# RWKV scan: the inverse of each tile built on its transpose alone, one 64x64 turn per level, on one Trainium2 core

## The chip, the cores and the metric

One core of one Trainium2 chip. The metric is the device time of one execution in microseconds (us), lower is better. The kernel before takes 3937.26 us, the median of 3 runs (3935.75 to 3940.57).

## What is computed

The reference is a two-layer model (D = 1024, 512 tokens and 256 context tokens, batch 1), all in float32. The change touches one part, the RWKV-7 scan of the first layer:

```python
def wkv7_scan(s0, r, w, kk, a, k, v):
    def step(s, inp):
        r_t, w_t, kk_t, a_t, k_t, v_t = inp
        s_kk = einsum('bhvk,bhk->bhv', s, kk_t)
        s = (s * w_t[:, :, None, :] - s_kk[..., None] * (kk_t * a_t)[:, :, None, :]
             + v_t[..., None] * k_t[:, :, None, :])
        return s, einsum('bhvk,bhk->bhv', s, r_t)
```

It runs over 16 heads of 64, in both directions of time: first over the 256 context tokens from a zero state, then over the 512 tokens from the state that the context left.

## The kernel before, in words

**Stages.** The kernel is a row of stages, each a block in which every engine has its own program and waits on named semaphores. Only `stage_rwkv_scan` (L666 to L1255) is touched. It lies between the key directions (L595) and the output of the mixer (from L1265).

**Tiles.** The scan works on 12 tiles of 128 tokens: tiles 0 to 3 are the context, 4 to 11 the tokens (`is_lat`). Even tiles run forward and odd ones backward. A tile holds 2 chunks of 64 tokens (`c` or `rows_of(c)`, the two halves of the 128 partitions) and 16 heads, which are kept in two groups `g` of 8. So every per-tile matrix of scores is 32 blocks of 64x64, in a tile buffer of 128 x 16 x 64.

**The inverse.** In each chunk the recurrence needs T = (I - A)^-1, where A is strictly triangular (its side depends on the direction). The kernel before forms A (`scores(kappa, beta, 0, n)`, L981) and its transpose AT (L983), in PSUM banks 0, 1 and 2, 3. `start_of_inverse` (L1105) cuts out of them the start of T and of its transpose TT for blocks of 2, and AT; GpSimd adds the identity to T and to TT (L1098, L1101). Five levels (`LEVELS`, blocks of 2, 4, 8, 16, 32) then double the block. One level is four steps:

- `level_product` (L824): per group 16 matmuls of 64x64x64, AT by T, into bank g.
- `level_mask` (L1121): VectorE multiplies the bank by the mask of this level's blocks and writes X.
- `level_change` (L837): per group 32 matmuls with 32 columns each, half of them for the change of T (L847, not on the last level) and half for the change of TT (L850).
- `level_update` (L1127): VectorE adds the change to T (not on the last level) and to TT, 256 columns each.

Group 1 of a step runs while VectorE works on group 0.

**Other work of a tile.** On TensorE: the scores BT, and QT and GT for `is_lat` tiles (`scores`, L809); 24 turns of 128x128 (`turn`, L818); the projections of the next tile (`prep_decay` L855, `prep_rate` L865, `prep_sums` L873); `b_times_v` (L884); state work of the tile before (`from_state`, `to_state`, and for `is_lat` tiles `output_from_state` and `output_from_tile`); at the end `kappa_times_t` (L957) and `t_times_bv` (L967). On ScalarE (L1038 to L1091), in this order: copies of the three turned matrices (L1042), tanh of the next tile's projections (L1047, L1051), the copy of b_times_v's result (`bv`, L1081), `prep_factor` (L1055, which releases `tmp_ready`), `prep_exp` (L1061), and the copies `tkt` (L1088) and `ub` (L1090). On VectorE, `prep_rates` (L1144) waits for `tmp_ready`.

**What sets the order.** Every engine's order of work is written out by hand: TensorE at L976 to L1036, VectorE at L1205 to L1255. Within an engine nothing overtakes. SyncE (L775) loads a tile's inputs; the load of tile n+2 starts when `featured` (L1167) says that VectorE has finished the features of tile n+1.

Of the kernel before, what the change touches and what calls it, by code (L numbers as in the profile page):

```python
# [665 lines left out]
def stage_rwkv_scan(k, y):  # L666
# [3 lines left out]
    LEVELS = (2, 4, 8, 16, 32)  # L670
# [4 lines left out]
    with ExitStack() as s:  # L675
# [17 lines left out]
        AT, BT, T, TT, X = (sb(n, [P, 2 * HP, C]) for n in ("AT", "BT", "T", "TT", "X"))  # L693
# [8 lines left out]
        a_ps, at_ps, bt_ps, qt_ps, gt_ps = sem("a_ps"), sem("at_ps"), sem("bt_ps"), sem("qt_ps"), sem("gt_ps")  # L702
        turned, tok_taken = sem("turned"), sem("tok_taken")
        t_off, tt_off, t_ready, tt_ready = sem("t_off"), sem("tt_off"), sem("t_ready"), sem("tt_ready")
# [64 lines left out]
        def side_of(m, b, side):  # L769
            return m.rearrange("p (n s b) -> p n s b", s=2, b=b)[:, :, side, :]  # L770

        BEFORE = ("c_before0", "c_before1")

        with nc.Block() as block:
# [33 lines left out]
            def _(pe):  # L808
# [27 lines left out]

                def level_change(n, l):  # L837
                    b, d = LEVELS[l], n % 2
                    for g in range(2):
                        need(pe, masked, 2 * NL * n + 2 * l + g + 1)  # L840
                        if l == 0:
                            need(pe, tt_ready, 2 * n + g + 1)
# [133 lines left out]
                for n in range(-1, TILES + 1):  # L976
                    now, nxt, prev = 0 <= n < TILES, n + 1 < TILES, n >= 1
                    if now:
                        need(pe, featured, n + 1)
                        need(pe, updated, 2 * NL * n)  # L980
                        scores(kappa, beta, 0, n).then_inc(a_ps, 1)  # L981
# [5 lines left out]
                        turn(ktil, 6)  # L987
                        need(pe, tok_taken, 3 * n + 1)
                        turn(kappa, 4)
                        level_product(n, 0)  # L990
                        need(pe, tt_off, 2 * n + 2)
                        scores(ktil, kappa, 2, n).then_inc(bt_ps, 1)
                        if is_lat(n):
                            need(pe, tok_taken, 3 * n + 2)
                            scores(beta, rr[n % 3], 6, n).then_inc(qt_ps, 1)
                        level_change(n, 0)
                    if nxt:
                        prep_decay(n + 1)
                    if now:
                        if is_lat(n):  # L1000
                            need(pe, bt_sb, n + 1)
                            scores(ktil, rr[n % 3], 2, n).then_inc(gt_ps, 1)
                        level_product(n, 1)
                    if nxt:
                        prep_rate(n + 1)
                    if now:
                        b_times_v(n)
                        level_change(n, 1)
                    if nxt:
                        prep_sums(n + 1)  # L1010
                    if now:
                        level_product(n, 2)
                    if prev:
                        from_state(n - 1, 0)
                    if now:
                        level_change(n, 2)
                    if prev:
                        to_state(n - 1, 0)
                    if now:
                        level_product(n, 3)  # L1020
                    if prev:
                        from_state(n - 1, 1)
                    if now:
                        level_change(n, 3)
                    if prev:
                        to_state(n - 1, 1)
                        if is_lat(n - 1):
                            output_from_state(n - 1)
                    if now:
                        level_product(n, 4)  # L1030
                        level_change(n, 4)
                    if prev and is_lat(n - 1):
                        output_from_tile(n - 1)
                    if now:
                        kappa_times_t(n)
                        t_times_bv(n)  # L1036
# [56 lines left out]
            @block.gpsimd  # L1093
            def _(pool):
                for n in range(TILES):
                    for g in range(2):
                        need(pool, t_off, 2 * n + g + 1)
                        pool.tensor_tensor(group(T, g), group(T, g), wide("c_ident", 0), ALU.add).then_inc(t_ready, 1)  # L1098
                    for g in range(2):
                        need(pool, tt_off, 2 * n + g + 1)  # L1100
                        pool.tensor_tensor(group(TT, g), group(TT, g), wide("c_ident", 0), ALU.add).then_inc(tt_ready, 1)  # L1101

            @block.vector
            def _(dve):
                def start_of_inverse(n):  # L1105
                    d = n % 2
                    need(dve, a_ps, n + 1)
                    for g in range(2):
                        dve.tensor_tensor(group(T, g), bank8(g), wide("c_off1", 1 - d), ALU.mult).then_inc(t_off, 1)
                    need(dve, at_ps, n + 1)  # L1110
                    for g in range(2):
                        dve.tensor_tensor(group(AT, g), bank8(2 + g), wide(BEFORE[d], 1), ALU.mult).then_inc(at_sb, 1)
                    for g in range(2):
                        dve.tensor_tensor(group(TT, g), bank8(2 + g), wide("c_off1", d), ALU.mult).then_inc(tt_off, 1)
# [12 lines left out]
                def level_update(n, l):  # L1127
                    b, d = LEVELS[l], n % 2
                    for g in range(2):
                        need(dve, change_ps, 2 * NL * n + 2 * l + g + 1)  # L1130
                        for m, side, at0 in ((T, d, 0), (TT, 1 - d, 256)):
                            if m is T and l == NL - 1:
                                continue
                            cols = group(m, g).rearrange("p h (n s b) -> p h n s b", s=2, b=b)[:, :, :, side, :]
                            change = k.ps[:, g, at0:at0 + 256].rearrange("p (h n b) -> p h n b", h=HP, b=b)
                            ins = dve.tensor_tensor(cols, cols, change, ALU.add)
                        ins.then_inc(updated, 1)
# [67 lines left out]
                for n in range(-1, TILES + 1):  # L1205
                    now, nxt, prev = 0 <= n < TILES, n + 1 < TILES, n >= 1
                    if now:
# [3 lines left out]
                        kept(BT[:, :, :], 2, n, 1, bt_sb)  # L1211
                        if is_lat(n):
                            need(dve, qt_ps, outputs(n))
                            kept(QT[:, n % 2, :, :], 6, n, 0, qt_sb)
                        level_update(n, 0)
# [3 lines left out]
                        level_mask(n, 1)  # L1219
# [6 lines left out]
                    if now:  # L1226
                        level_mask(n, 2)
                    if prev:
                        add_from_state(n - 1, 0)
                    if now:  # L1230
                        level_update(n, 2)
# [4 lines left out]
                    if now:  # L1236
                        level_mask(n, 3)
# [4 lines left out]
                    if now:  # L1242
                        level_update(n, 3)
                    if nxt:
                        prep_rr(n + 1)
                    if now:
                        level_mask(n, 4)
                    if prev:
                        new_state(n - 1, 1)
                    if nxt:  # L1250
                        prep_ktil(n + 1)
                    if now:
                        level_update(n, 4)
                    if prev and is_lat(n - 1):
                        add_output(n - 1)  # L1255

# [2269 lines left out]
```

## Time and profile before

| | |
|---|---|
| median of 3 runs | 3937.26 us |
| the profiled execution | 3941.41 us |
| its span, first to last instruction | 3939.4 us |
| TensorE busy in the span | 3295.8 us (84%) |
| VectorE busy | 1126.9 us (29%) |
| ScalarE / GpSimd busy | 542.5 / 166.5 us |
| mean granted TensorE clock | 0.903 of full |
| the scan, 465 to 1180 us of the span | 715 us |

PE is TensorE's matmul side, PEld its weight load, DVE VectorE, ACT ScalarE, POOL GpSimd, SP SyncE; a trailing q is an engine's sequencer. One float32 matmul of the program stands in the trace as two MATMUL records with a LDWEIGHTS each, one transpose as one. The time in brackets at the end of a row is how long the engine sat idle before it, and what released it; "issue" is a wait for nothing that the profile shows.

### The profile page before, as it was taken

The numbers are of one execution on the slowest core, as the hardware profiler recorded it, in microseconds if no ns is written. First come the engines' busy times: TensorE is split into PE (matmuls) and PEld (weight loads), VectorE is DVE, ScalarE is ACT, GpSimd is POOL, SyncE is SP. The second block draws the span as 40 slices with busy tenths as digits, with TensorE's granted clock in tenths as the row PEclk, the third lists the DMA queues.
The fourth block names the chain that finished last, engine by engine and source line by source line (L and its number), as shares of the span: only waits on it lengthen the run. The fifth ranks groups of instructions, "written<-read, shape, count | busy, mean of one in ns | idle before, by whom it ended". The sixth has DMA issues, their size and how long they took to land. (4 is left out here: it accounts for less than half of the span.)

```text
span 3939.4 us, 75830 instructions
## 1 busy us (share of the span) xinstructions
PE 3295.8 (84%) x34311; PEld 2300.8 (58%) x34311; DVE 1126.9 (29%) x1926; ACT 542.5 (14%) x995; POOL 166.5 (4%) x167
## 2 busy tenths in 40 slices
PE   3898599989988899998599999995796678887774
PEld 1354488988882344444399999894344444544442
DVE  1301455655545211134511111012103473201102
ACT  0001222222202100001100010100101131100001
POOL 0000011010100000000100000001000010100000
PEclk8899699999997899998799999997896589899997
DMA  7722311011103122471467778661300011899994
GB/s 310 218 71 74 89 48 48 26 48 46 29 19 129 43 64 85 113 271 44 145 226 265 266 249 280 232 225 65 104 25 1 21 38 79 340 427 426 427 427 180
DMA packets 246763, 613.04 MB, mean 156 GB/s; under 512 B 27188, under 2 KB 136278, under 8 KB 230968
## 3 DMA queue, kind: packets, MB, share of 16 engines
q1 hardware_dynamic: 219720, 531.05, 37.0%
q10 hardware_dynamic: 15968, 54.41, 3.6%
q0 software_dynamic: 10768, 22.87, 1.9%
q8 instruction: 268, 4.39, 0.5%
q14 instruction: 39, 0.32, 0.0%
HBM read 565.64 MB, written 42.63 MB: 154 GB/s over the span
## 5 line engine op out<-in xcount | busy, mean ns | idle before, releaser
L2667 PE MATMUL ps<-moe_xt,moe_wb 128*128 128x152 f32 (+1 forms) x3520 | 456.6, 292 | 2.3 <-DVE moe_xt L2829 2.3
L2667 PEld LDWEIGHTS ps<-moe_xt,moe_wb 128*128 128x128 f32 x3520 | 451.9, 193 | 2.9 <-issue 2.1
L1633 PE MATMUL ps<-ffn_h,ffn_wb 128*128 128x512 f32 x704 | 304.2, 595 | 15.5 <-PEq L1539 15.5
L2347 PE MATMUL ps<-hier_wb,hier_xt 128*64 128x256 f32 x2048 | 244.3, 394 | 75.0 <-DMA hier_wb<-in_expert_w_up 43.7
L2347 PEld LDWEIGHTS ps<-hier_wb,hier_xt 128*64 128x64 f32 x2048 | 160.9, 142 | 170.1 <-issue 64.5
L1633 PEld LDWEIGHTS ps<-ffn_h,ffn_wb 128*128 128x128 f32 x704 | 134.4, 191 | 185.3 <-issue 185.3
L2674 PE MATMUL ps<-moe_hT,moe_wb 128*128 128x152 f32 (+1 forms) x1760 | 227.2, 290 | 0.0
L2674 PEld LDWEIGHTS ps<-moe_hT,moe_wb 128*128 128x128 f32 x1760 | 222.7, 190 | 0.0
L850 PE MATMUL ps<-TT,X 64*64 64x32 f32 x3840 | 213.2, 220 | 3.2 <-issue 2.3
L850 PEld LDWEIGHTS ps<-TT,X 64*64 64x64 f32 x3840 | 197.7, 136 | 4.5 <-issue 3.3
L847 PE MATMUL ps<-X,TT 64*64 64x32 f32 x3072 | 188.3, 220 | 3.7 <-issue 3.1
L847 PEld LDWEIGHTS ps<-X,TT 64*64 64x64 f32 x3072 | 173.9, 136 | 4.1 <-issue 2.9
L1702 PE MATMUL ps<-ffn_g,ffn_wd 128*128 128x512 f32 x352 | 153.0, 598 | 2.6 <-PEq L1605 2.6
L2363 PE MATMUL ps<-hier_wb,hier_actT 128*64 128x512 f32 x512 | 116.9, 598 | 17.0 <-DMA hier_wb<-in_expert_w_down 12.3
L833 PE MATMUL ps<-T,AT 64*64 64x64 f32 x3840 | 127.3, 219 | 0.0
L833 PEld LDWEIGHTS ps<-T,AT 64*64 64x64 f32 x3840 | 119.9, 134 | 7.1 <-issue 5.7
L2950 PE MATMUL ps<-in_u,in_wb 128*128 128x512 f32 x256 | 113.0, 604 | 10.0 <-PEq L2877 10.0
L1702 PEld LDWEIGHTS ps<-ffn_g,ffn_wd 128*128 128x128 f32 x352 | 67.4, 192 | 88.2 <-issue 88.2
L2833 DVE SCALAR_TENSOR_TENSOR moe_th<-moe_th,ps 128x152 f32<-128x152 f32 (+1 forms) x110 | 33.9, 308 | 286.1 <-ACT moe_th L2767 286.1
L462 DVE SCALAR_TENSOR_TENSOR mix<-xx,vec,h 128x768 f32<-128x768 f32 (+1 forms) x48 | 43.6, 969 | 203.3 <-PE ps L530 152.7
L1124 DVE TENSOR_TENSOR X<-ps,sq 128x512 f32<-128x512 f32 x120 | 81.2, 689 | 65.3 <-PE ps L833 63.5
L1661 DVE SCALAR_TENSOR_TENSOR ffn_th<-ffn_th,ps 128x512 f32<-128x512 f32 x22 | 15.2, 689 | 273.1 <-ACT ffn_th L1646 273.1
(486 smaller groups left out, 4129.6 us busy)
## 6 DMA issues: line engine op xcount, KB each, us to landing
moe_wb<-in_moe_w SPq DMA_DIRECT2D x60, 2048.0 KB, 10.3
hier_wb<-in_expert_w_gate SPq DMA_DIRECT2D x32, 2048.0 KB, 37.8
hier_wb<-in_expert_w_up SPq DMA_DIRECT2D x32, 2048.0 KB, 37.5
hier_wb<-in_expert_w_down SPq DMA_DIRECT2D x32, 2048.0 KB, 38.4
moe_wb<-in_moe_w SPq DMA_DIRECT2D x30, 1536.0 KB, 8.1
wb_ada<-in_ada_w SPq DMA_DIRECT2D x8, 3072.0 KB, 18.6
ada_late<-in_ada_w ACTq DMA_DIRECT2D x8, 3072.0 KB, 9.6
ffn_wb<-in_ffn_w SPq DMA_DIRECT2D x22, 1024.0 KB, 7.8
```

Source lines behind the costliest of these rows:

```text
L462: return dve.scalar_tensor_tensor(mix[:, n % 2, c, own], xx[:, c, own], k.v(f"mu{order[n]}")[:, c:c + 1], h[:, c, own], ALU.mult, ALU.add)
L833: mm = pe.matmul(k.ps[rows_of(c), g, q * C:(q + 1) * C], AT[rows_of(c), g * HP + q, :], T[rows_of(c), g * HP + q, :], start=True, stop=True)
L847: pe.matmul(k.ps[rows_of(c), g, q * 32:(q + 1) * 32], TT[rows_of(c), at, :], side_of(X[rows_of(c), at, :], b, d), start=True, stop=True)
L850: mm = pe.matmul(k.ps[rows_of(c), g, 256 + q * 32:256 + (q + 1) * 32], X[rows_of(c), at, :], side_of(TT[rows_of(c), at, :], b, 1 - d), sta ...
L1124: dve.tensor_tensor(group(X, g), bank8(g), wide(f"c_off{LEVELS[l]}", 1 - n % 2), ALU.mult).then_inc(masked, 1)
L1633: mm = pe.matmul(k.ps[:, bank + q, :], wb[:, j, q, c, o * P:(o + 1) * P], h[:, c, :], start=c == 0, stop=c == KC - 1)
L1702: mm = pe.matmul(k.ps[:, j, :], wd[:, j, c, :], g[:, c, :], start=c == 0, stop=c == FC - 1)
L2347: mm = pe.matmul(k.ps[both_halves(a), bank, 0:256], xs[:, c, :], wb[:, slot, at:at + 256], start=c == 0, stop=c == KC - 1)
L2363: mm = pe.matmul(k.ps[both_halves(a), 7, :], at_sb[:, c, :], wb[:, slot, at:at + 512], start=c == 0, stop=c == 3)
L2667: mm = pe.matmul(k.ps[:, bank, 0:width], wb[:, slot, at:at + P], xs[:, c, :], start=c == 0, stop=c == KC - 1)
L2674: mm = pe.matmul(out_columns(o, width), wb[:, slot, at:at + P], hT[:, f, 0:width], start=f == 0 and o % 3 == 0, stop=f == FC - 1 and (o % ...
L2950: mm = pe.matmul(k.ps[:, e % 6, :], own[:, piece] if kind == "fm" else tokens[:, piece], tokens if kind == "fm" else own, start=c == 0, st ...
```

## The change

The change drops T and keeps the recursion on AT alone. Six levels (blocks of 1 to 32) now do the same four steps: turn the current AT (`level_turn`: for the first half of the partitions a transpose, for the second a matmul with the identity), mask the turned matrix into X, multiply X by AT into the bank (64 columns a block), and add the whole bank to AT. The last level adds to TT, which GpSimd has filled with AT + I after level 4. The scores A, the start of T and TT, and GpSimd's additions to T go. The hand-written orders of TensorE and VectorE are rearranged around the six levels; ScalarE's is not.

```diff
-    LEVELS = (2, 4, 8, 16, 32)
+    LEVELS = (1, 2, 4, 8, 16, 32)
...
-                def level_product(n, l):
+                def level_turn(n, l):
                     for g in range(2):
                         if l == 0:
                             need(pe, at_sb, 2 * n + g + 1)
-                            need(pe, t_ready, 2 * n + g + 1)
                         else:
                             need(pe, updated, 2 * NL * n + 2 * (l - 1) + g + 1)
                         for q in range(HP):
-                            for c in range(2):
-                                mm = pe.matmul(k.ps[rows_of(c), g, q * C:(q + 1) * C], AT[rows_of(c), g * HP + q, :],
-                                               T[rows_of(c), g * HP + q, :], start=True, stop=True)
+                            cols, m, one = slice(q * C, (q + 1) * C), AT[:, g * HP + q, :], k.square("c_ident")[:, 0:C]
+                            pe.transpose(k.ps[rows_of(0), g, cols], m[rows_of(0), :], one[rows_of(0), :])
+                            mm = pe.matmul(k.ps[rows_of(1), g, cols], m[rows_of(1), :], one[rows_of(1), :], start=True,
+                                           stop=True)
                         mm.then_inc(x_ps, 1)
...
                         for q in range(HP):
                             at = g * HP + q
-                            if l < NL - 1:
-                                for c in range(2):
-                                    pe.matmul(k.ps[rows_of(c), g, q * 32:(q + 1) * 32], TT[rows_of(c), at, :],
-                                              side_of(X[rows_of(c), at, :], b, d), start=True, stop=True)
                             for c in range(2):
-                                mm = pe.matmul(k.ps[rows_of(c), g, 256 + q * 32:256 + (q + 1) * 32],
-                                               X[rows_of(c), at, :], side_of(TT[rows_of(c), at, :], b, 1 - d),
-                                               start=True, stop=True)
+                                mm = pe.matmul(k.ps[rows_of(c), g, q * C:(q + 1) * C], X[rows_of(c), at, :],
+                                               AT[rows_of(c), at, :], start=True, stop=True)
                         mm.then_inc(change_ps, 1)
```

TensorE's order of a tile after the change, with the functions' names (those in brackets only where the tile, or the one before, is an `is_lat` one):

```text
scores AT (waits ub_taken of the tile before), turn beta, turn ktil, level_turn 0, turn kappa,
scores BT, level_change 0, [scores QT], prep_decay, level_turn 1, [scores GT], prep_rate,
level_change 1, b_times_v, level_turn 2, prep_sums, level_change 2, from_state 0, level_turn 3,
to_state 0, level_change 3, from_state 1, level_turn 4, to_state 1, level_change 4,
[output_from_state], level_turn 5, [output_from_tile], level_change 5, kappa_times_t, t_times_bv
```

GpSimd and VectorE:

```diff
                 for n in range(TILES):
+                    need(pool, ub_ps, n)
                     for g in range(2):
-                        need(pool, t_off, 2 * n + g + 1)
-                        pool.tensor_tensor(group(T, g), group(T, g), wide("c_ident", 0), ALU.add).then_inc(t_ready, 1)
-                    for g in range(2):
-                        need(pool, tt_off, 2 * n + g + 1)
-                        pool.tensor_tensor(group(TT, g), group(TT, g), wide("c_ident", 0), ALU.add).then_inc(tt_ready, 1)
+                        need(pool, updated, 2 * NL * n + 2 * (NL - 2) + g + 1)
+                        pool.tensor_tensor(group(TT, g), group(AT, g), wide("c_ident", 0), ALU.add).then_inc(tt_ready, 1)
...
                 def level_update(n, l):
-                    b, d = LEVELS[l], n % 2
                     for g in range(2):
                         need(dve, change_ps, 2 * NL * n + 2 * l + g + 1)
...
+                        if l == NL - 1:
+                            need(dve, tt_ready, 2 * n + g + 1)
+                        m = group(AT if l < NL - 1 else TT, g)
+                        dve.tensor_tensor(m, m, bank8(g), ALU.add).then_inc(updated, 1)
```

In VectorE's order `level_update` 2 to 5 and `level_mask` 3 to 5 each have a place of their own. `prep_rates` still stands between `level_update` 1 and `level_mask` 2, `prep_rr` and `prep_ktil` now stand between `level_update` 4 and `level_mask` 5, and `level_update` 5 comes last, behind `add_output`.

## Rows read from the trace of the kernel before

**Rows 1.** The scan as one stretch: us, busy of PE, PEld, DVE, ACT, POOL; PEclk, DMA, GB/s.
```profile
465.00:1180.00 715.00, 653.25 (x20960) 617.63 (x20960) 395.34 (x648) 174.94 (x325) 59.92 (x48) 0.95 0.15 39
```

**Rows 2.** Groups by line, 429 to 1190 us: count, busy, mean ns, idle before.
```profile
L850 PE MATMUL ps<-TT,X 64*64 64x32 f32 x3840 | 213.2, 220 | 3.2 <-issue 2.3 <-DVE X L1124 0.9
L847 PE MATMUL ps<-X,TT 64*64 64x32 f32 x3072 | 188.3, 220 | 3.7 <-issue 3.1 <-DVE X L1124 0.6
L1124 DVE TENSOR_TENSOR X<-ps,sq 128x512 f32<-128x512 f32 x120 | 81.2, 689 | 65.3 <-PE ps L833 63.5
L814 PE MATMUL ps<-x 64*64 64x64 f32 x2304 | 51.9, 243 | 30.6 <-issue 21.4 <-DVEq L1167 8.2 <-ACT ub L1090 0.9
```

**Rows 3.** Timeline of TensorE: start, length, line, count.
```profile
940.85 1.16 PE L814 MATMUL ps<-rr,x 64*64 64x64 f32 x64
...
588.37 2.08 PE L892 MATMUL ps<-V,BT 64*64 64x64 f32 x64
594.09 2.06 PE L879 MATMUL ps<-sq,lw 64*128 64x128 f32 x32
```

**Rows 4.** Timeline of ScalarE in tile 2, same columns.
```profile
590.76 1.02 ACT L1081 ACTIVATE bv<-ps 128x1024 f32<-128x1024 f32 x1
591.68 3.17 ACT L1057 ACTIVATE x<-x,kar,kah 128x128 f32<-128x128 f32 x8
```

**Rows 5.** Timeline of VectorE in tile 2.
```profile
592.34 0.42 DVE L1136 TENSOR_TENSOR T<-T,ps 128x256 f32<-128x256 f32 x1 [3.65 <-PE ps L850]
...
594.20 0.42 DVE L1136 TENSOR_TENSOR T<-T,ps 128x256 f32<-128x256 f32 x1 [1.11 <-PE ps L850]
...
594.98 1.23 DVE L1147 SCALAR_TENSOR_TENSOR x<-x,rkk 128x1024 f32<-128x1024 f32 x1
...
597.42 1.47 DVE L1124 TENSOR_TENSOR X<-ps,sq 128x512 f32<-128x512 f32 x2
...
616.87 1.22 DVE L1166 TENSOR_TENSOR x<-x 128x1024 f32<-128x1024 f32 x1
```

**Rows 6.** Timeline at the end of tile 1 and the start of tile 2.
```profile
565.14 1.99 PE L963 MATMUL ps<-TT,tok_kappa 64*64 64x64 f32 x64 [2.25 <-DVE TT L1136]
...
569.68 1.02 ACT L1090 ACTIVATE ub<-ps 128x1024 f32<-128x1024 f32 x1 [1.47 <-PE ps L972]
...
570.76 1.16 PE L814 MATMUL ps<-x 64*64 64x64 f32 x64 [0.19 <-ACT ub L1090]
```

**Rows 7.** Timeline of TensorE at the end of tile 5 and start of tile 7.
```profile
789.69 1.16 PE L963 MATMUL ps<-TT,tok_kappa 64*64 64x64 f32 x64 [0.79 <-DVE TT L1136]
...
859.50 2.61 PE L814 MATMUL ps<-x 64*64 64x64 f32 x83 [3.20 <-issue]
862.04 4.46 PE L820 MATMUL ps<-sq,x 128*128 128x128 f32 x24
```

**Rows 8.** Busy time by stretch in a tile's middle and at two tile starts.
```profile
603.00:606.00 3.00, 3.00 (x110) 3.00 (x108) 2.92 (x5) 0.00 (x0) 0.00 (x0) 1.00 0.02 5
...
729.00:732.00 3.00, 0.76 (x50) 0.76 (x53) 2.07 (x4) 0.00 (x0) 0.00 (x0) 1.00 0.02 6
732.00:735.00 3.00, 3.00 (x82) 3.00 (x76) 0.00 (x0) 1.02 (x1) 0.00 (x0) 0.55 1.02 277
...
858.00:861.00 3.00, 1.50 (x57) 1.50 (x60) 0.56 (x1) 0.00 (x0) 0.00 (x0) 0.60 0.81 239
...
864.00:867.00 3.00, 3.00 (x35) 2.83 (x35) 0.63 (x2) 2.36 (x3) 2.51 (x2) 0.77 0.03 5
```

**Rows 9.** VectorE's first instruction of tiles 2, 3, 7 and 8.
```profile
570.65 1.29 DVE L1109 TENSOR_TENSOR T<-ps,sq 128x512 f32<-128x512 f32 x2 [5.57 <-PE ps L814]
...
624.59 1.29 DVE L1109 TENSOR_TENSOR T<-ps,sq 128x512 f32<-128x512 f32 x2 [5.63 <-PE ps L814]
...
860.44 1.29 DVE L1109 TENSOR_TENSOR T<-ps,sq 128x512 f32<-128x512 f32 x2 [7.21 <-PE ps L814]
...
921.96 1.29 DVE L1109 TENSOR_TENSOR T<-ps,sq 128x512 f32<-128x512 f32 x2 [6.92 <-PE ps L814]
```

More of the change, by code:

```diff
@@ L692, in stage_rwkv_scan @@
         tok_b, tok_k, tok_kappa = sb("tok_b", [P, 2, D]), sb("tok_k", [P, 2, D]), sb("tok_kappa", [P, D])
-        AT, BT, T, TT, X = (sb(n, [P, 2 * HP, C]) for n in ("AT", "BT", "T", "TT", "X"))
+        AT, BT, TT, X = (sb(n, [P, 2 * HP, C]) for n in ("AT", "BT", "TT", "X"))
         QT, GT = (sb(n, [P, 2, 2 * HP, C]) for n in ("QT", "GT"))
@@ L979, in _ @@
                         need(pe, featured, n + 1)
-                        need(pe, updated, 2 * NL * n)
-                        scores(kappa, beta, 0, n).then_inc(a_ps, 1)
                         need(pe, ub_taken, n)
@@ L987, in _ @@
                         turn(ktil, 6)
+                        level_turn(n, 0)
                         need(pe, tok_taken, 3 * n + 1)
                         turn(kappa, 4)
-                        level_product(n, 0)
-                        need(pe, tt_off, 2 * n + 2)
+                        need(pe, at_sb, 2 * n + 2)
                         scores(ktil, kappa, 2, n).then_inc(bt_ps, 1)
+                        level_change(n, 0)
                         if is_lat(n):
@@ L999, in _ @@
                     if now:
+                        level_turn(n, 1)
                         if is_lat(n):
@@ L1006, in _ @@
                     if now:
+                        level_change(n, 1)
                         b_times_v(n)
-                        level_change(n, 1)
+                        level_turn(n, 2)
                     if nxt:
@@ L1011, in _ @@
                     if now:
-                        level_product(n, 2)
+                        level_change(n, 2)
                     if prev:
@@ L1015, in _ @@
                     if now:
-                        level_change(n, 2)
+                        level_turn(n, 3)
                     if prev:
@@ L1019, in _ @@
                     if now:
-                        level_product(n, 3)
+                        level_change(n, 3)
                     if prev:
@@ L1023, in _ @@
                     if now:
-                        level_change(n, 3)
+                        level_turn(n, 4)
                     if prev:
                         to_state(n - 1, 1)
-                        if is_lat(n - 1):
-                            output_from_state(n - 1)
                     if now:
-                        level_product(n, 4)
                         level_change(n, 4)
+                    if prev and is_lat(n - 1):
+                        output_from_state(n - 1)
+                    if now:
+                        level_turn(n, 5)
                     if prev and is_lat(n - 1):
@@ L1034, in _ @@
                     if now:
+                        level_change(n, 5)
                         kappa_times_t(n)
@@ L1105, in start_of_inverse @@
                 def start_of_inverse(n):
[L1106 to L1109, printed above, removed]
                     need(dve, at_ps, n + 1)
                     for g in range(2):
-                        dve.tensor_tensor(group(AT, g), bank8(2 + g), wide(BEFORE[d], 1), ALU.mult).then_inc(at_sb, 1)
-                    for g in range(2):
-                        dve.tensor_tensor(group(TT, g), bank8(2 + g), wide("c_off1", d), ALU.mult).then_inc(tt_off, 1)
+                        dve.tensor_tensor(group(AT, g), bank8(2 + g), wide(BEFORE[n % 2], 1), ALU.mult).then_inc(at_sb, 1)
                 def kept(dst, banks, n, side, ready):
@@ L1227, in _ @@
                         level_mask(n, 2)
+                        level_update(n, 2)
                     if prev:
@@ L1242, in _ @@
                     if now:
[L1243 to L1246, printed above, removed]
                         level_mask(n, 4)
@@ L1249, in _ @@
                         new_state(n - 1, 1)
+                    if now:
+                        level_update(n, 4)
                     if nxt:
+                        prep_rr(n + 1)
                         prep_ktil(n + 1)
                     if now:
-                        level_update(n, 4)
+                        level_mask(n, 5)
                     if prev and is_lat(n - 1):
                         add_output(n - 1)
+                    if now:
+                        level_update(n, 5)
 def load_projection(k, sp, wb, w):
```

26 lines of the change are left out of this document (6 added, 20 removed).

## The prediction

> **What bounds the kernel now.** I first read the busy time by stretch. The scan takes 715 us, TensorE is busy in 653 of them, VectorE in 395, and the clock granted is 0.95 of full [rows 1]. So TensorE's stream of instructions is the bound, and what counts is how long that stream is and where it stands still. In the middle of a tile it has no gap: 3.00 of 3.00 us busy at clock 1.00, from 603 us on [rows 8]. It stands still at the tile boundaries. The timeline shows three kinds of gap there. One is a wait for VectorE before kappa_times_t, 2.25 us in tiles whose predecessor has no output and 0.79 us in the others [rows 6, 7]. One is a short wait for the ub copy, 0.19 us [rows 6]. The third is "issue", up to 3.20 us [rows 7], and 21.4 + 2.3 + 3.1 = 26.8 us in the three largest groups [rows 2]. After most gaps of over 2 us the clock falls for some us: 0.55 behind the gap at 729, 0.60 behind the one before 859 [rows 8]. A tile lasts 53.9 us in the context (570.65 to 624.59) and 61.5 us later on (860.44 to 921.96) [rows 9].
>
> **The price of a small matmul.** All prices below are for full clock. 64 records of scores take 1.16 us, 64 of b_times_v 2.08 us [rows 3]; without the 0.22 us that the last one needs to finish (the mean length in rows 2) that is 14.5 and 29 ns a record. The difference between the two is in the code: scores use all four pairings of partition halves (in and out), b_times_v two (c with c). So a record holds its own quarter of the array for about 58 ns, and what runs in another quarter costs nothing beside it. The level steps are of the second kind. In level_change group 1 follows group 0 by 594.20 - 592.34 = 1.86 us for 64 records of 32 columns [rows 5]. That is also 29 ns, so 32 columns are no cheaper than 64. I count in units of 64 records on two quarters, 1.87 us.
>
> **TensorE's work.** Before, a tile has 5 products of one unit, 4 changes of two and a last one of one: 14 units, 26.2 us, and the scores A, 64 records of the cheap kind, 0.93 us. After, the change is one unit a level. A turn has one record in the first quarter (the transpose) and two in the last (the identity matmul) for each pair of blocks. Counted by records it would be 3 x 29 = 88 ns a pair, counted by its busier quarter 2 x 58 = 117 ns. I take 117, since rows 3 fit the quarters, and a turn is then a unit as well. After: 12 units, 22.4 us. Saved: 26.2 + 0.93 - 22.4 = 4.7 us a tile, **56 us** over 12 tiles. Bounds: at 88 ns a turn takes 1.4 us and 6 x 12 turns give 32 us more; if each transpose runs alone for 58 ns, 6 x 12 x 16 of them cost 67 us.
>
> **VectorE** loses 4 of 6 instructions of start_of_inverse (4 x 0.69), gains one mask (2 x 0.69), and 18 updates of 0.42 become 12 of 0.69: about 0.6 us a tile less, at the mean of rows 2 and the length in rows 5. It isn't the bound, and its total doesn't matter. GpSimd's two instructions run under turn 5. No transfer is added or removed. What matters is who waits for whom.
>
> **The new wait in the middle, +43 us.** ScalarE's order is unchanged: the bv copy waits for b_times_v, prep_factor comes behind it, and VectorE's prep_rates waits for that. In tile 2 b_times_v ends at 590.45. The copy starts at 590.76, the factor at 591.68, it is done at 594.85, and prep_rates starts at 594.98 [rows 3, 4, 5]. Level 2's mask, behind it in VectorE's order, starts at 597.42 and takes 0.69. So level_change 2 cannot start before 598.2. Today level_change 1 (3.7 us), prep_sums (594.09 + 2.06 - 590.45 shows both, 5.7 us), product 2 and from_state 0 (1.87 + 0.94) fill this time: 8.5 us of cover for 7.7. After the change level_change 1 stands ahead of b_times_v, and only turn 2 (1.87) and prep_sums (1.98) are left between. TensorE stands still for 7.7 - 3.85 = 3.9 us, in every tile that prepares another: 11 x 3.9 = 43 us. Bounds: 3.4 and 4.2 a tile (the copy starts 0.3 us sooner or VectorE 0.2 us later).
>
> **The ub copy, +13 us.** AT's scores write the banks that hold t_times_bv's result, so they wait for the copy of 1.02 us. Today the scores A run in that time and 0.19 us is left [rows 6]. With A gone the whole 0.2 + 1.02 + 0.1 us shows: 1.15 us more, 11 times.
>
> **The end of a tile, +9 us.** In tiles 1 to 4 (no outputs of the tile before to run) prep_rr and prep_ktil, 2.5 us of VectorE by rows 5, now stand between update 4 and mask 5. TensorE has only turn 5 in this time: about 3.0 us of waits before turn 5 and level_change 5, and 1.0 us before kappa_times_t (0.24 + 0.69 + 0.1). That takes the place of the 2.25 us: +1.75 x 4 = 7. In the other tiles output_from_tile covers the masks, and 1.0 takes the place of 0.79: +2.
>
> **Issue waits, -25 us.** They stand behind long runs of cheap records (two or three of 64 at 14.5 ns) and where the DMA share is 1.2 [rows 7, 8]. My reading is that the instructions themselves arrive too slowly there; it is a reading, the trace names no releaser. The change breaks up these runs: A goes, level_change 0 comes between BT and QT, level_change 5 between output_from_tile and kappa_times_t. The new semaphore waits at the boundary let instructions pile up too. Bounds: all 27 us go or none.
>
> **The clock, +3 us.** 0.05 of 715 us is 36 us of work lost. I expect a fall behind each 3.9 us wait, as behind the gaps of rows 8, and fewer at the boundaries. A fall costs 1.5 to 2 us. Between 18 fewer and 37 us more (11 falls at up to 3.4), I take +3.
>
> **Sum:** -56 + 43 + 13 + 9 - 25 + 3 = -13 us. The profiled execution took 3941.4 us, its span 3939.4; it gives 3928. The median before is 4.1 lower, 3937.3, so I predict **3924 us** against it. 0.2% (8 us) is about what a measurement of this kernel can tell from no change.
>
> **A rule that speaks against it.** During 24 transposes in a row, 862.04 to 866.5, the granted clock came back from 1.2 GHz, and the stretch from 864 us already shows 0.77 [rows 7, 8]; so transposes don't hold the clock down here. The Trainium skill (TensorE: Matmul & The Clock Gate, Part 4: PE-mode transpose) says that transpose mode doesn't count as activity for the clock gate in the way matmuls do. By that rule the trace doesn't agree.
>
> **The rivals.**
> - *Slower, 3953 us.* The falls of the clock. The wait of 3.9 us before level_change 2 brings a fall in each tile, and the boundary waits (1.0 + 1.3 us, plus issue) keep theirs. That is 11 x 1.7 = 19 us more than before, in place of 3, and with the runs at the boundary still dense, half of the issue waits stay (+13). -13 + 16 + 13 = +16. It decides as soon as the mean clock of the scan falls below 0.93. For it: in rows 8 a fall follows both gaps. Against it: the boundary waits come in pieces. 20%.
> - *No change, 3938 us.* The issue waits only move: they need time, not order, and about 12 us of them go instead of 25. 15%.
> - *Faster, 3897 us.* Turns run at the rate of records, 88 ns a pair: -32, of which the 5 us in turn 2 lie under the wait, so -27. For it: one record less in the busy stream. Against: rows 3. The same time results if the clock stays up and the ub wait hides under issue. 20%.
> - *Transposes run alone, 3980 us.* +67 us, less the 11 of turn 2. Against: the transposes at 862.04 start before the matmuls ahead of them end, at 862.11 [rows 7]. 4%.
> - *The turns pull the clock down, about 4050 us.* The six turns of each tile (6 x 1.87 x 12 = 135 us) run at 1.2 GHz throughout and take twice as long, less what waits cover. Against: rows 7 and 8 above. 1%. It is what the rule of the Trainium skill named above (TensorE: Matmul & The Clock Gate) would make of the turns.
>
> **Chances.** My forecast has 40%, with its own range 3910 to 3936. Within it about three in four lie below 3929, so faster by over 0.2% is 0.30 + 0.20 = 0.50. No change is 0.10 + 0.11 = 0.21. The rest is slower: 0.29. The range of 8 in 10 reaches from 3890 (the turn at its low bound) to 3965 (both of the slower rival's terms at full size).
>
> **What would show it.** Right: the scan's matmul records fall by 3456 to about 17500. Groups of changes and of turns follow each other by 0.93 us. VectorE's first instruction of prep_rates waits for ScalarE in each tile, and TensorE is idle by 3.5 to 4.2 us before level_change 2. The first scores of a tile wait 1.3 us for ub. The context tiles last 54 to 56 us, the later ones 57 to 59. Wrong: the wait before level_change 2 under 2 us, turns closer than 0.8 us, issue waits as large as now, or the stages after the scan changed at all.

## The result, and the profile after

The changed kernel takes **4450.07 us** (median of 4 runs, 4448.43 to 4463.19) against 3938.91 us for the kernel before in the same batch (the three runs of above and one more): a ratio of 1.131 (95% interval 1.129 to 1.133). That is 511 us slower. The prediction said 3924 us and gave the range 3890 to 3965, so it was wrong in sign and in size. The profiled execution has a span of 4461.4 us.

The page of the changed kernel, busy time and the 40 slices:

```profile
PE 3845.5 (86%) x30855; PEld 2649.8 (59%) x30855; DVE 1146.0 (26%) x1830; ACT 542.7 (12%) x995; POOL 136.8 (3%) x143
...
PEclk8997676677767677899997899999879659899997
```

Fewer matmul records (30855, the 3456 fewer that were forecast), and 550 us more of busy TensorE. The clock is low in the slices of the scan. Busy time by stretch, the scan as one stretch, to be set beside [rows 1], both up to the first work of the next stage:

```profile
465.00:1707.00 1242.00, 1207.99 (x17508) 969.35 (x17508) 416.80 (x553) 176.35 (x327) 30.42 (x24) 0.71 0.09 24
```

The scan takes 1242 us instead of 715 (522 us more, when both are measured to the start of its last instruction, at 1696.15 and at 1174.14), with the clock at 0.71 instead of 0.95. TensorE has hardly a gap. So it is no wait of the kind that the prediction counted. The groups by line, 429 to 1700 us, show where the time went (to be set beside [rows 2]):

```profile
L830 PE MATMUL ps<-sq,AT 64*64 64x64 f32 x2304 | 449.7, 285 | 0.0
L829 PE MATMUL ps<-sq,AT 64*64 64x64 f32 x1152 | 312.5, 271 | 0.0
L840 PE MATMUL ps<-AT,X 64*64 64x64 f32 x4608 | 225.3, 274 | 0.0
L1106 DVE TENSOR_TENSOR X<-ps,sq 128x512 f32<-128x512 f32 x144 | 99.6, 692 | 427.7 <-PE ps L830 426.8
```

L829 is the transpose of a turn, L830 the identity matmul beside it. They have fewer records than the changes of L840 and take over three times as long, and VectorE's masks wait 427 us for L830. The timeline of TensorE in a turn of tile 5 (start, length, line, count):

```profile
996.42 0.24 PE L829 MATMUL ps<-sq,AT 64*64 64x64 f32 x1
996.59 0.33 PE L830 MATMUL ps<-sq,AT 64*64 64x64 f32 x2
996.85 0.24 PE L829 MATMUL ps<-sq,AT 64*64 64x64 f32 x1
...
999.73 0.31 PE L829 MATMUL ps<-sq,AT 64*64 64x64 f32 x1
999.97 0.47 PE L830 MATMUL ps<-sq,AT 64*64 64x64 f32 x2
1000.37 0.31 PE L829 MATMUL ps<-sq,AT 64*64 64x64 f32 x1
```

From transpose to transpose it is 0.43 us at full clock (996.42 to 996.85) and 0.64 us at half (999.73 to 1000.37). The prediction took 0.117 us. The matmul starts 0.17 us behind the start of the transpose, and the next transpose 0.26 us behind that of the matmul pair. Matmul records alone, on two quarters, follow each other by 0.029 us. And the clock falls inside the turn (us, busy time of the engines, PEclk before the last two numbers):

```profile
996.00:999.00 3.00, 3.00 (x23) 2.09 (x21) 0.00 (x0) 3.00 (x9) 0.00 (x0) 0.97 0.00 0
999.00:1002.00 3.00, 3.00 (x16) 1.86 (x15) 2.46 (x3) 0.35 (x1) 0.00 (x0) 0.50 0.03 8
```

TensorE counts as busy for 3.00 of 3.00 us in both rows, with 23 and 16 records where the middle of a tile had 110 [rows 8]. "Busy" here is the length of the records, 0.24 us each and more, and not the rate at which they follow.

### The profile page after: what moved, and what is told of

The parts are those of the page before. It is cut to its first block and busy times, and to the rows that moved or that the text cites. A ratio compares the mean times of both kernels' runs of the same rounds, so it can differ in the third digit from the quotient of the medians.

```text
span 4461.4 us, 68782 instructions
## 1 busy us (share of the span) xinstructions
PE 3845.5 (86%) x30855; PEld 2649.8 (59%) x30855; DVE 1146.0 (26%) x1830; ACT 542.7 (12%) x995; POOL 136.8 (3%) x143
## 5 line engine op out<-in xcount | busy, mean ns | idle before, releaser
L830 PE MATMUL ps<-sq,AT 64*64 64x64 f32 x2304 | 449.7, 285 | 0.0
L830 PEld LDWEIGHTS ps<-sq,AT 64*64 64x64 f32 x2304 | 265.1, 161 | 100.8
L829 PE MATMUL ps<-sq,AT 64*64 64x64 f32 x1152 | 312.5, 271 | 0.0
L840 PE MATMUL ps<-AT,X 64*64 64x64 f32 x4608 | 225.3, 274 | 0.0
L840 PEld LDWEIGHTS ps<-AT,X 64*64 64x64 f32 x4608 | 215.8, 185 | 4.8 <-issue 4.3
L1106 DVE TENSOR_TENSOR X<-ps,sq 128x512 f32<-128x512 f32 x144 | 99.6, 692 | 427.7 <-PE ps L830 426.8
L829 PEld LDWEIGHTS ps<-sq,AT 64*64 64x64 f32 x1152 | 131.9, 115 | 109.5 <-issue 10.4
L1115 DVE TENSOR_TENSOR AT<-AT,ps 128x512 f32<-128x512 f32 x120 | 82.2, 686 | 113.8 <-PE ps L840 113.4
```

Of the source, the lines that this page charges most:

```text
L829: pe.transpose(k.ps[rows_of(0), g, cols], m[rows_of(0), :], one[rows_of(0), :])
L830: mm = pe.matmul(k.ps[rows_of(1), g, cols], m[rows_of(1), :], one[rows_of(1), :], start=True, stop=True)
L840: mm = pe.matmul(k.ps[rows_of(c), g, q * C:(q + 1) * C], X[rows_of(c), at, :], AT[rows_of(c), at, :], start=True, stop=True)
L1106: dve.tensor_tensor(group(X, g), bank8(g), wide(f"c_off{LEVELS[l]}", 1 - n % 2), ALU.mult).then_inc(masked, 1)
L1115: dve.tensor_tensor(m, m, bank8(g), ALU.add).then_inc(updated, 1)
```

## The experiments

**1. The turn by matmuls alone.** Both halves of the partitions use the identity matmul, everything else as in the change.

```diff
+                        one = k.square("c_ident")[:, 0:C]
                         for q in range(HP):
-                            cols, m, one = slice(q * C, (q + 1) * C), AT[:, g * HP + q, :], k.square("c_ident")[:, 0:C]
-                            pe.transpose(k.ps[rows_of(0), g, cols], m[rows_of(0), :], one[rows_of(0), :])
-                            mm = pe.matmul(k.ps[rows_of(1), g, cols], m[rows_of(1), :], one[rows_of(1), :], start=True,
-                                           stop=True)
+                            for c in range(2):
+                                mm = pe.matmul(k.ps[rows_of(c), g, q * C:(q + 1) * C], AT[rows_of(c), g * HP + q, :],
+                                               one[rows_of(c), :], start=True, stop=True)
```

> The change, but both halves of the partitions are turned by the identity matmul; no transpose is left in level_turn. Theory S (each switch between transpose and matmul empties TensorE: a pair of one transpose and one matmul takes 0.43 us at full clock in the profile of the change, against 0.117 us for two matmuls): a turn becomes a unit of 1.87 us and the time falls to what the prediction's sum said, 3924 us (3905 to 3945), with the scan's mean clock back at 0.93 or more. Rival L (the turn is slow because it waits on something else, AT's update or the bank): the turns stay near 10 us and the time above 4300. In both cases the wait before level_change 2 should now show: under S 3.9 us in 11 tiles.

3953.3 us (3948.4 to 3956.7, 6 runs), 1.0033 times the kernel before (1.0021 to 1.0046). So 497 of the 511 us belong to the 1152 transposes, 0.43 us for each. (That this is also the length of a pair at full clock is chance: a pair of matmuls takes 0.117 of it anyway, and the rest of the 0.43 is told apart below.) Rival L falls. A turn is a unit, as the sum had it: 64 records take 2.08 us in the row below. But the time is 29 us above the forecast, outside what was expected, and the clock of the scan is 0.92, where 0.93 or more was. The timeline of TensorE and then of VectorE in tile 6 shows the waits that the prediction had worked out:

```profile
815.51 0.41 PE L811 MATMUL ps<-x 64*64 64x64 f32 x11 [1.21 <-ACT ub L1080]
...
821.93 2.08 PE L830 MATMUL ps<-sq,AT 64*64 64x64 f32 x64
...
846.20 3.36 PE L840 MATMUL ps<-AT,X 64*64 64x64 f32 x58 [3.59 <-DVE X L1106]
```

```profile
843.02 1.23 DVE L1125 SCALAR_TENSOR_TENSOR x<-x,rkk 128x1024 f32<-128x1024 f32 x1 [5.39 <-ACTq L1049]
844.16 1.22 DVE L1126 TENSOR_TENSOR x<-x,rkk 128x1024 f32<-128x1024 f32 x1
845.45 1.29 DVE L1106 TENSOR_TENSOR X<-ps,sq 128x512 f32<-128x512 f32 x2
```

VectorE waits 5.39 us for ScalarE's factor, runs prep_rates, then the mask, and TensorE stands still for 3.59 us (forecast 3.9) before level_change 2. The change behind it, 58 records in 3.36 us, then starts at the low clock; 58 records of the change at 800.36 took 1.86. The scan's stretch and the largest waits of TensorE (in total, times, longest):

```profile
465.00:1193.00 728.00, 616.43 (x18658) 580.85 (x18658) 413.87 (x553) 176.23 (x327) 30.02 (x24) 0.92 0.14 39
```

```profile
PE ps L840 <- DVE X L1106: 59.4, 22, 3.6
PE ps L811 <- ACT ub L1080: 13.3, 11, 1.2
PE ps L952 <- DVE TT L1115: 9.5, 12, 0.8
```

**2. The transposes in blocks.** The same transposes and matmuls as in the change, but 8 transposes first and 8 matmuls behind them in each group.

```diff
+                        one = k.square("c_ident")[:, 0:C]
                         for q in range(HP):
-                            cols, m, one = slice(q * C, (q + 1) * C), AT[:, g * HP + q, :], k.square("c_ident")[:, 0:C]
-                            pe.transpose(k.ps[rows_of(0), g, cols], m[rows_of(0), :], one[rows_of(0), :])
-                            mm = pe.matmul(k.ps[rows_of(1), g, cols], m[rows_of(1), :], one[rows_of(1), :], start=True,
-                                           stop=True)
+                            pe.transpose(k.ps[rows_of(0), g, q * C:(q + 1) * C], AT[rows_of(0), g * HP + q, :],
+                                         one[rows_of(0), :])
+                        for q in range(HP):
+                            mm = pe.matmul(k.ps[rows_of(1), g, q * C:(q + 1) * C], AT[rows_of(1), g * HP + q, :],
+                                           one[rows_of(1), :], start=True, stop=True)
```

> The change, but in each group the 8 transposes come first and the 8 matmuls behind them: 2 switches a group in place of 16. Theory S (the cost is the switch, 0.18 + 0.25 us for each transpose and its matmul): a group takes 8 x 0.06 + 8 x 0.12 + 2 x 0.2 = 1.8 us instead of 3.4, a turn 3.6 us; 72 turns at 1.75 us over a unit are 126 us, so about 4050 us (4000 to 4110). Rival T (a 64x64 transpose is slow by itself, about 0.2 us each wherever it stands): a group takes 8 x 0.18 + 8 x 0.12 = 2.4 us or more and the time is 4150 or more.

3995.0 us in one run, 455 us less than the change with the same instructions. TensorE's timeline in one turn, and the scan's stretch:

```profile
800.67 0.63 PE L829 MATMUL ps<-sq,AT 64*64 64x64 f32 x8
801.24 1.14 PE L832 MATMUL ps<-sq,AT 64*64 64x64 f32 x16
802.31 0.63 PE L829 MATMUL ps<-sq,AT 64*64 64x64 f32 x8
```

```profile
465.00:1220.00 755.00, 681.81 (x17294) 629.40 (x17296) 411.79 (x542) 175.04 (x325) 29.96 (x24) 0.96 0.13 35
```

A block of 8 transposes takes 0.57 us to the next start. At 0.058 us each that leaves 0.11 us for the switch, and 1.07 - 16 x 0.058 leaves 0.14 us for the switch back. A group takes 1.64 us, where rival T asked for 2.4 or more. So a transpose isn't slow by itself (rival T falls), the switch is. The same prices give the alternating pair: 0.06 for the transpose, 0.11, 0.12 for its matmul, 0.14, together 0.43 us. The clock stays at 0.96. The time is 55 us below what I expected, and below the expected range, for which I had a turn at 3.6 us and nothing that covers it. Against experiment 1 it is 42 us more. 72 turns of 3.3 instead of 1.87 us make 101, the waits before the changes fall from 59.4 to 35.5 us (before level_change 2 from 3.6 to 2.2 a time), and the higher clock gives back about 28 by (1 - clock) x time.

**3. Half of the turns.** Levels 1, 3 and 5 by matmuls, levels 0, 2 and 4 alternating.

```diff
...
-                            pe.transpose(k.ps[rows_of(0), g, cols], m[rows_of(0), :], one[rows_of(0), :])
...
+                            if l % 2 == 0:
+                                pe.transpose(*turned_block)
+                            else:
+                                pe.matmul(*turned_block, start=True, stop=True)
...
```

> The change, but levels 1, 3 and 5 are turned by matmuls alone; levels 0, 2 and 4 keep the alternating transposes. If the loss is in proportion to the number of alternating turns: half of it goes, about 4190 us (4160 to 4220). If the clock is what matters beyond the switches and it recovers once the slow turns stand apart: the scan's mean clock is well over the middle between 0.71 and 0.95, and the time lower, 4120 to 4160. If it stays down for the whole tile: over 4220.

4185.9 us in one run, 233 above experiment 1 for 576 transposes: 0.40 us each, against 0.43 for all of them. The loss is nearly in proportion, as the first of the three expectations had it. The scan's clock is 0.81, about halfway between 0.71 and 0.92: setting the slow turns apart doesn't rescue it beyond their share.

**4. The wait before level_change 2.** On top of experiment 1, prep_rates goes behind level_update 2 in VectorE's order.

```diff
-                    if nxt:
-                        prep_rates(n + 1)
                     if now:
                         level_mask(n, 2)
                         level_update(n, 2)
+                    if nxt:
+                        prep_rates(n + 1)
```

> The kernel with matmul turns (3953 us), and prep_rates moved behind level_update 2 in VectorE's order. Theory W (what that kernel loses against the sum is the wait of 3.6 us before level_change 2 in 11 tiles, and a fall of the clock behind each): the wait goes, TensorE runs through to to_state 0, 40 us go, and with the falls behind them 50 to 60: 3893 to 3913 us, mean clock of the scan 0.95 or more. Rival M (the wait moves on, to the mask of level 3 or to prep_kappa, since VectorE and ScalarE have the same work to do): 3935 to 3950, with a new wait of 2 to 3 us on TensorE before level_change 3.

3912.2 us (3909.7 to 3916.4), 0.9926 times the kernel before (0.9906 to 0.9946), and 41 us less than experiment 1. TensorE's waits:

```profile
PE ps L840 <- DVE X L1106: 21.2, 11, 3.6
...
PE ps L897 <- DVE N L1163: 9.0, 11, 1.6
...
PE ps L917 <- DVE ub L1151: 6.6, 11, 0.6
```

The 38 us before level_change 2 are gone. What remains before L840 is mostly the tail of tiles 0 to 4, five waits of about 3.5 us. 14 us of new waits stand before from_state 1 and to_state, so rival M is right in small part. 38 - 14 = 24 us of the 41 are waits; the scan's clock is back at 0.95, and by difference the rest is its part.

**5. The ub copy.** On top of 4, AT's scores stand behind the turn of beta.

```diff
-                        need(pe, ub_taken, n)
-                        scores(beta, kappa, 2, n).then_inc(at_ps, 1)
                         need(pe, tkt_taken, n)
                         turn(beta, 4)
+                        need(pe, ub_taken, n)
+                        scores(beta, kappa, 2, n).then_inc(at_ps, 1)
```

> As the one before, and the scores of AT stand behind the turn of beta, which fills 0.93 of the 1.2 us for which they wait for the ub copy. If each of the waits counts for itself: 11 x 0.9 = 10 us less than the one before, some 0.1 of it lost again at AT's masks. If the waits for instructions only take their place: within 3 us of it.

3904.1 us (3889.2 to 3905.5): 8 us less, where 10 were expected. The runs of the two kernels just fail to overlap, so the size is rough.

**6. The tail.** On top of 5, level_mask 5 stands ahead of prep_rr and prep_ktil.

```diff
-                    if nxt:
-                        prep_rr(n + 1)
-                        prep_ktil(n + 1)
                     if now:
                         level_mask(n, 5)
+                    if nxt:
+                        prep_rr(n + 1)
+                        prep_ktil(n + 1)
```

> As the one before, and level_mask 5 stands ahead of prep_rr and prep_ktil in VectorE's order. The waits before level_change 5 are in the tiles 1 to 4 only (about 3 us each at prep_rr's old length, 4 with the 2.1 us that it takes in these kernels): 8 to 14 us less than the one before. If update 5, now behind prep_ktil, becomes late instead: no gain, and a longer wait before kappa_times_t (over 1.5 us).

**3878.7 us** (3876.2 to 3882.2), 0.9842 times the kernel before (0.9821 to 0.9863): the fastest kernel of this study, 1.6% faster than before. It gains 25 us over experiment 5 where 8 to 14 were expected. Of the waits before L840 (20.9 us in experiment 5) 2.2 us are left, and kappa_times_t now waits 22.8 us where it waited 9.5, up to 2.9 us at a time. So these waits explain only 19 - 13 = 5 us of the gain. The scan's clock rises from 0.94 to 0.97, and (1 - clock) x time from about 41 to 20 us; that is most of it, by estimate. What a wait of the tail cost beyond itself shows in experiment 5, in tile 3:

```profile
671.55 3.68 PE L840 MATMUL ps<-AT,X 64*64 64x64 f32 x64 [3.59 <-DVE X L1106]
676.02 1.98 PE L952 MATMUL ps<-TT,tok_kappa 64*64 64x64 f32 x64 [0.79 <-DVE TT L1115]
```

At full clock these take 2.08 and 1.16 us (at 808.35 and 811.27 in experiment 1). VectorE's multiplication in prep_rr is shorter as well, in experiment 1 and here (min, median and max in ns); no run shows that this by itself shortened the kernel:

```profile
L1141 DVE TENSOR_TENSOR rr<-rr,rkk x12: 1225/2136/2142, 463.2 to 1111.4; 128x1024 f32<-128x1024 f32 x12
```

```profile
L1141 DVE TENSOR_TENSOR rr<-rr,rkk x12: 1224/1226/1226, 464.1 to 1046.8; 128x1024 f32<-128x1024 f32 x12
```

**7. GpSimd's additions later.** On top of experiment 1 alone, GpSimd's two additions for TT wait until VectorE has finished the next tile's features.

```diff
                         need(pool, updated, 2 * NL * n + 2 * (NL - 2) + g + 1)
+                        if n + 1 < TILES:
+                            need(pool, featured, n + 2)
```

> The kernel with matmul turns (3953 us), but GpSimd's two additions wait until VectorE has finished the next tile's features. prep_rr's multiplication takes 2.14 us in the kernels with the change against 1.23 before. If GpSimd's additions, which run at the same time, are what slows it: 1.23 us again in all 12, and pend's copies short again. If it is something else (the place in the order, the clock): still 2.1. The time hardly moves (3945 to 3960), since the additions now come closer to update 5.

3921.1 us in one run, 32 us less than experiment 1, with prep_rr's multiplication at 1.226 us again. So GpSimd is what slows it: in experiment 1 the additions run from 802.76 to 805.27 in tile 5, and VectorE's multiplication from 804.22 takes 2.14 us. That the time would hardly move was wrong. VectorE is spared about 19 us, in the multiplications and in the copies ahead of them, but all of TensorE's waits in the scan together fall only from 114 to 108 us. The scan's clock is 0.94 instead of 0.92, some 15 us by (1 - clock) x time; the rest I did not track down, and it is one run.

**8. Both.** Experiment 6 with GpSimd's later additions.

> The kernel with matmul turns, later rates, the ub order and the tail order (3879 us), and GpSimd's additions wait for the next tile's features. In that kernel prep_rr already takes 1.23 us, since the additions run beside other work. If what GpSimd slows is only prep_rr: nothing to gain, and TT comes 1 to 2 us later in each tile, so 3885 to 3900. If it also slows what stands beside it now (masks, prep_ktil): 3865 to 3875.

3894.1 us (3892.1 to 3897.3), 15 us slower than experiment 6. In experiment 6 the additions no longer run beside prep_rr, so there is nothing to gain, and TT comes late: the waits before kappa_times_t grow from 22.8 to 37.7 us.

**9 and 10. The switch in the kernel before.** 960 extra transposes in level_product, whose result the matmul behind them overwrites; nothing else differs from the kernel before. In 9 each stands ahead of its pair of matmuls; 10 has the last added line as well, so that eight stand ahead of each group.

```diff
                         for q in range(HP):
+                            pe.transpose(k.ps[rows_of(0), g, q * C:(q + 1) * C], AT[rows_of(0), g * HP + q, :],
+                                         k.square("c_ident")[rows_of(0), 0:C])
+                        for q in range(HP):
                             for c in range(2):
```

> The kernel BEFORE the change, with one extra 64x64 transpose ahead of each pair of matmuls in level_product: 960 transposes, whose result the matmul behind them overwrites; nothing else differs. Theory S (each switch between transpose and matmul empties TensorE): each costs 0.3 us at full clock and 0.43 with the falls of the clock that came with them in the change, 300 to 410 us, so 4240 to 4350 us. Rival (the loss in the change came from its other new order, not from alternation): 960 x 0.06 = 58 us at most, 3940 to 4000.

> As the one before, the same 960 transposes, but 8 of them in a row ahead of each group's 16 matmuls: 240 switches in place of 1920. Theory S: 960 x 0.06 + 240 x 0.12 = 86 us, 4010 to 4040, with the clock as before (0.95 in the scan). If a transpose is dear by itself: near the alternating kernel. If transposes in a row don't count as activity for the clock: a mean clock under 0.92.

Alternating: 4543.7 us, 605 more than before, even beyond what was expected. In blocks: 4021.0 us, 82 more (86 worked out). TensorE's timeline in experiment 9, at full clock and at half:

```profile
495.44 0.24 PE L832 MATMUL ps<-sq,AT 64*64 64x64 f32 x1
495.61 0.33 PE L835 MATMUL ps<-T,AT 64*64 64x64 f32 x4
495.87 0.24 PE L832 MATMUL ps<-sq,AT 64*64 64x64 f32 x1
...
804.29 0.31 PE L832 MATMUL ps<-sq,AT 64*64 64x64 f32 x1
804.53 0.48 PE L835 MATMUL ps<-T,AT 64*64 64x64 f32 x4
804.94 0.31 PE L832 MATMUL ps<-sq,AT 64*64 64x64 f32 x1
```

Its scan as one stretch (busy times of the engines, PEclk before the last two numbers):

```profile
465.00:1780.00 1315.00, 1273.77 (x21920) 1059.37 (x21920) 402.33 (x652) 174.80 (x325) 59.94 (x48) 0.66 0.08 22
```

TensorE's timeline in experiment 10:

```profile
811.88 0.63 PE L832 MATMUL ps<-sq,AT 64*64 64x64 f32 x8
812.44 1.15 PE L836 MATMUL ps<-T,AT 64*64 64x64 f32 x32
```

Its scan as one stretch:

```profile
465.00:1260.00 795.00, 730.70 (x21927) 678.58 (x21928) 402.21 (x651) 176.92 (x328) 59.87 (x48) 0.96 0.14 38
```

Same instructions, same operands, 1920 switches against 240, and 523 us between them. The order of the change plays no part here, so the switch alone is enough. At full clock it is 0.17, 0.26 and 0.43 us again, as in the change, though a transpose here writes where the matmul behind it writes, and there it didn't: the place of the output isn't the reason. 9 costs 0.63 us a transpose, of which 0.43 - 0.117 = 0.31 are the switches at full clock and the transpose itself. The rest comes with the clock: a mean of 0.66 between the two levels means 1.2 GHz in about two thirds of the scan, and the falls also slow the work that has no switches, the changes and the state work.

## Why the prediction was wrong, point by point

**The step that failed** is the price of the turn: "I take 117, since rows 3 fit the quarters, and a turn is then a unit as well." It holds for matmuls beside matmuls (experiment 1: 497 us less). For a transpose beside a matmul it was taken from rows in which none stood. A pair takes 0.43 us at full clock, 0.25 of it in the two switches. 1152 x (0.43 - 0.117) = 361 us is the part of the alternation at full clock. What is left is by difference. TensorE's waits in the scan add up to 114 us in experiment 1 and to 36 in the change, whose long turns cover the others. So 497 - 361 + 78 = 214 us go to the clock, 0.71 against 0.92. That is an estimate; no run holds the clock fixed.

**The bound was wrong too.** The sum had "if each transpose runs alone for 58 ns, 6 x 12 x 16 of them cost 67 us". That priced a transpose without overlap, and not the standstill on both sides of it. The rival built on it had 4% and 3980 us. Its argument against was that "the transposes at 862.04 start before the matmuls ahead of them end, at 862.11". That is true and proves nothing, since each record is 0.22 us long and more while the next starts 0.0145 to 0.117 us behind it: all records overlap. The distance between starts had to be read. It was there in the kernel before, around the 128x128 turns at the start of tile 8:

```profile
922.71 0.91 PE L814 MATMUL ps<-x 64*64 64x64 f32 x25
923.54 1.97 PE L820 MATMUL ps<-sq,x 128*128 128x128 f32 x16
925.75 1.09 PE L820 MATMUL ps<-sq,x 128*128 128x128 f32 x8 [0.24 <-ACT tok_b L1042]
926.78 0.92 PE L833 MATMUL ps<-T,AT 64*64 64x64 f32 x24
```

The last score starts at 922.71 + 0.91 - 0.22 = 923.40, the first transpose at 923.54: 0.14 us, where scores follow by 0.029 at the 1.2 GHz of this stretch. The last transpose starts at 925.75 + 1.09 - 0.27 = 926.57, the first matmul 0.21 us later, where transposes follow by 0.117. That leaves 0.11 and 0.09 us for the switches. With these, and the 0.058 us for which a transpose that overlaps nothing holds TensorE, 1152 pairs take 300 us more, and a forecast of about 4220 us could have been made from the kernel before, still without the clock. It would have been an estimate: these turns also change the tile, from 64*64 to 128*128 and back, and the rows price both changes together.

**The rule weighed against the trace.** Transposes in a row did not hold the clock down: 0.96 in the scans of experiments 2 and 10, with 1152 and 960 of them in runs of 8, half a microsecond each, and it had come back during the 24 in a row of [rows 7, 8]. No longer run was tried. So the rule of the Trainium skill (TensorE: Matmul & The Clock Gate, Part 4: PE-mode transpose), that transposes don't count like matmuls, is not what these runs show, as far as they reach. Its result, a clock pulled down in the turns, did come when transposes alternated with matmuls. I gave it 1%. The Trainium skill has a nearer rule that I did not weigh (TensorEngine Tiling (Array Packing), Tiling Modes, Key Properties): changing the tiling mode drains TensorE. Experiment 9 shows a standstill of this kind between a transpose and matmuls for which the trace gives the same tile, 64*64. What TensorE does in that time, the trace doesn't show, and only float32 was tried.

**The rest of the sum**, tested in experiment 1, where -13 us was forecast and +14 measured:
- The work saved, -56 us: right as far as it can be read. A turn has the length of a unit and the record counts are as forecast.
- The wait in the middle, +43: right. 3.59 us against 3.9, 39 us in 11 tiles; taking it away gave 41 us, the clock's part included (experiment 4).
- The ub copy, +13: right. The kernel before waits there for 0.9 us in all, here it is 13.3 us in 11 waits.
- The tail, +9: too small. 59.4 - 11 x 3.6 = 20 us stand mostly before level_change 5 of tiles 0 to 4 (I had 1 to 4), about 3.5 us each. With 9.5 us before kappa_times_t, and 11.8 there in the kernel before, that is +18. prep_rr takes 2.14 us instead of 1.23, since GpSimd adds at the same time; I had costed GpSimd at nothing ("run under turn 5").
- Issue waits, -25: TensorE's sum falls from 36 to 17 us, so -19.
- The clock, +3: wrong. (1 - 0.92) x 728 = 58 us of work lost against 36, so about +22. That is the "slower" rival's mechanism at its own mark, a mean clock below 0.93.

With the measured terms the sum is -56 + 39 + 12 + 18 - 19 + 22 = +16, against +14. So apart from the turn, two terms were mis-sized, the clock by 19 us and the tail by 9.

## What to carry to other kernels

Don't alternate TensorE transposes and matmuls. Put transposes in blocks, or turn small tiles by the identity matmul like their neighbours. When a trace doesn't show two kinds of instruction alternating, look for the one place where they meet and compare the distance between starts there with the distance within a kind. And when a change shortens one engine's stream, walk the other engines' hand-written orders again: moving three pieces of work was worth 75 us here, more than the 56 of the saved instructions. Part of the 75 is the clock, which fell behind the waits that went.

## What the runs showed of the hardware that I had not expected

- A switch between float32 transposes and matmuls of 64x64 on TensorE costs 0.11 us in one direction and 0.14 back at full clock. A transpose and a matmul in alternation take 0.43 us (0.06 + 0.11 + 0.12 + 0.14), and 0.64 us at 1.2 GHz.
- The granted clock fell to 1.2 GHz behind a stretch of 3 us that the profile calls 100% busy, with 23 records in it, and stayed there through the next, with 16.
- GpSimd's additions slow a multiplication of VectorE with both inputs in SBUF from 1.23 to 2.14 us. The masks and updates beside the additions, which read PSUM, keep their 0.69 us.
